# Attention stage of a hybrid decoder layer on eight cores: the dilation groups in reverse order, the value blocks spread to the end, the normalisation by token blocks

## The chip, the cores and the metric

One Trainium2 chip; the same program runs on 8 cores, each on its own 2048 of the 16384 tokens, with the 2048 tokens ahead of them as a halo. No data passes between the cores. The time is the device time of the slowest core in microseconds. Engines: PE is TensorE (PEld its weight loads), DVE is VectorE, ACT is ScalarE, POOL is GpSimd, SP is SyncE, which only starts transfers.

## The reference, cut to what matters

Three groups of four heads attend with a window of 128, 512 or 2048 positions and a dilation of 1, 4 or 16: each query sees 129 keys of its own residue stream. The three groups are merged by their softmax denominators, which is one sum of numerators over one sum of denominators.

```
ATTN_GROUPS = ((128, 1), (512, 4), (2048, 16))  # (window, dilation) per head group
...
        for gi, (window, dilation) in enumerate(ATTN_GROUPS):
            hs = slice(gi * HEADS_PER_GROUP, (gi + 1) * HEADS_PER_GROUP)
            o_g, lse_g = dilated_window_attention(q[:, :, hs], k[:, :, hs], v[:, :, hs], window, dilation)
...
        wts = jax.nn.softmax(jnp.stack(lses, axis=0), axis=0)  # (G, B, S, Hg)
        o_attn = jnp.sum(wts[..., None] * jnp.stack(outs, axis=0), axis=0)
        y_pool = multiscale_pool(u, w_pool_mix[l], pool_scale[l])
        merged = gate_a * (o_attn @ w_proj_attn[l]) + gate_p * (y_pool @ w_proj_pool[l])
        x = x + rms_norm(merged @ w_out[l], g_post_mix[l])
```

A SwiGLU feed-forward layer follows.

## The kernel before, in words

The program is written out by hand: `pe.op`, `act.op`, `dve.op` and `pool.op` put an instruction at the end of their engine's own list, each engine runs its list in that order, and `waits=` makes an instruction wait for events of others. So an instruction that waits holds up all that stands behind it on its engine.

The stages of a core, in order: load and normalise x (`own_tick`), transpose it to `hT`; keys and queries with rotary embedding (`rope_unit`: eight matmuls at L438, a copy on ACT, a rotation matmul at L482, two products on DVE at L485 and L487, a sum on POOL at L498 into `qT` or `kT`, laid out by residue stream, so that POOL reads its inputs with a step of 4 or 16 elements for the dilated groups); the attention stage; the gated merge (L925 to L947); the output projection with its norm (L988); the feed-forward layer (L1144 to L1176).

The attention stage is the loop over `u`. A **unit** is a group `g`, a part `s_`, a half and a head pair `pr`; there are 48, 16 for each group. Step `u` of the loop puts out:

- `att_scores(u)`: 8 score matmuls into one of two bank pairs (L770), the exponential on ACT into a tile `PT` (L774, 128x1024), the mask product on DVE (L779).
- some **value blocks** (`v_own`: 8 matmuls at L518 in one of two banks, an eviction on ACT at L522), taken from `v_list` in the order of the groups.
- parts of the pooling branch: window sums and means of channel half 0 on DVE (`c0_steps`), window sums of half 1 on POOL in two runs of four instructions (`h10[0]`, `h11[0]`), their means on DVE (`h10[1]`, `h11[1]`, L709), and `pool_mix`, one matmul (L731) and one ACT instruction (L733).
- `att_apply(u - 2)`: 12 matmuls (L792, L797) into one of two banks; the first group is then copied into `acc` by ACT (L812), the others are added to `acc` by DVE (L815). The next use of that bank waits for this.

`acc` holds numerator and denominator in token order, so the dilated groups write it with a step of 4 or 16 floats. `att_norm` turns one pair's denominators of 512 tokens into reciprocals by a logarithm and an exponential on ACT (L830, L831) and multiplies (L832) into `oT2`, which the merge reads. The buffer `PT2` and `acc` lie where rope's tables, its temporaries and its weights were; therefore ACT and DVE wait ahead of the stage for all of PE's, DVE's and POOL's rope work.

## Time and profile before

| | |
|---|---|
| median of 3 runs | 1025.14 us (1024.16 to 1026.15) |
| the profiled execution, its own time | 1024.68 us |
| its span, on core 2, the slowest | 1023.1 us (the other cores from 1013.3) |
| PE busy | 930.6 us, 91% of the span |
| DVE, ACT, POOL busy | 39%, 33%, 33% |
| chain that ended last | PE 80%; DVE 5%; DMA 4%; issue 4%; POOL 3%; ACT 3% |
| attention stage on core 2 | from the first value matmul at 222.07 us to the first merge matmul at 336.22 us |

The span runs from the first to the last instruction of the slowest core; the device time is 1.6 us longer. PE is busy for nearly all of the second half; the stages in which it isn't are the first 110 us and the attention stage. "PEclk" is the clock granted to TensorE as a share of the full one (2.4 GHz; the lower level is 1.2 GHz).

### The profile page before, as it was taken

Reading aid. Unit: us, or ns where it says so; the run is one execution under the profiler, and the core shown is the slowest. Engines: PE = TensorE matmul, PEld = TensorE weight load, DVE = VectorE, ACT = ScalarE, POOL = GpSimd, SP = SyncE. Lnnn points to the kernel's source line nnn. Section 1 sums busy time; section 2 is a strip of 40 time slices with the busy share of each in tenths; the row PEclk is TensorE's granted clock in tenths of the full one; section 3 lists DMA queues with packets and bytes.
Section 4 is the critical chain, followed back from the end, with each engine's and each line's share of the span. In section 5 each row is a group of like instructions: output and inputs, shape, how many; then the busy total and the mean of one; then the engine's idle time right before and its main releaser. Section 6 shows DMA issues by size and latency. Waiting matters only on the chain.

```text
span 1023.1 us, 15111 instructions; the slowest of 8 cores (1013.3 to 1023.1 us)
## 1 busy us (share of the span) xinstructions
PE 930.6 (91%) x5448; PEld 468.4 (46%) x5532; DVE 402.5 (39%) x554; ACT 342.2 (33%) x588; POOL 334.7 (33%) x324
## 2 busy tenths in 40 slices
PE   1569999999897999999898999999999999999993
PEld 0337554447674444444444444444444444444441
DVE  2465786548978433333576212121112112121111
ACT  3426663339777422223664111111101111111100
POOL 2462787663402343333456111111333000000331
PEclk9769999999998999999999999999999999999997
DMA  8879310000022171212977766762334544530322
GB/s 233 243 173 239 80 63 21 1 1 2 4 41 43 43 124 21 42 21 42 304 240 194 118 108 117 122 108 49 124 105 139 86 71 74 83 62 1 124 104 81
DMA packets 32586, 98.50 MB, mean 96 GB/s; under 512 B 4224, under 2 KB 4224, under 8 KB 32512
## 3 DMA queue, kind: packets, MB, share of 16 engines
q0 software_dynamic: 15296, 41.92, 24.8%
q1 hardware_dynamic: 17072, 55.58, 16.3%
q8 instruction: 45, 0.74, 0.3%
q14 instruction: 29, 0.24, 0.1%
q10 hardware_dynamic: 144, 0.03, 0.0%
HBM read 122.64 MB, written 16.78 MB: 136 GB/s over the span
## 4 chain that ended last, share of the span: by engine, by line
PE 80%; DVE 5%; DMA 4%; issue 4%; POOL 3%; ACT 3%; SPq 0%; DVEq 0%; ACTq 0%; POOLq 0%
PE ps L1176 14%; PE ps L1147 14%; PE ps L1144 14%; PE ps L438 12%; PE ps L925 6%; PE ps L928 5%; PE ps L518 5%; DMA xst<-xh 2%; PE ps L988 2%; PE ps L420 2%; PE ps L935 1%; PE ps L932 1%; PE ps L482 1%; DMA xin<-xo 1%; DVE tb L996 1%
## 5 line engine op out<-in xcount | busy, mean ns | idle before, releaser
L1144 PE MATMUL ps<-hT,wgu 128*128 128x512 bf16 x658 | 157.5, 379 | 1.5 <-DMA wgu<-wgu 0.7
L1147 PE MATMUL ps<-hT,wgu 128*128 128x512 bf16 x659 | 157.6, 379 | 0.7
L1176 PE MATMUL ps<-wdn,ffT 128*128 128x512 bf16 x690 | 151.5, 379 | 2.6 <-DVE ffT L1159 1.9
L1159 DVE TENSOR_TENSOR ffT<-ps,sa 128x512 bf16<-128x512 f32 x88 | 60.8, 691 | 226.2 <-PE ps L1147 226.2
L1158 ACT ACTIVATE sa<-ps 128x512 f32<-128x512 f32 x88 | 52.5, 597 | 247.3 <-PE ps L1144 247.3
L1176 PEld LDWEIGHTS ps<-wdn,ffT 128*128 128x128 bf16 x704 | 68.8, 98 | 85.4 <-issue 2.8
L1144 PEld LDWEIGHTS ps<-hT,wgu 128*128 128x128 bf16 x672 | 65.6, 98 | 79.8 <-issue 1.2
L1147 PEld LDWEIGHTS ps<-hT,wgu 128*128 128x128 bf16 x672 | 65.8, 98 | 79.3
L74 POOL DMA_DIRECT2D wgu<-wgu x42 | 22.5, 537 | 231.9 <-PE ps L1147 228.3
L1001 POOL TENSOR_TENSOR x1b<-tb,xin 128x1024 f32<-128x1024 f32 x31 | 72.8, 2348 | 58.3 <-DVE tb L996 29.9
L438 PE MATMUL ps<-hT,wqk 128*128 128x512 bf16 x374 | 89.4, 379 | 2.0 <-DVE uh L631 1.4
L498 POOL TENSOR_TENSOR kT<-t,t2b 128x512 bf16<-128x512 f32 (+1 forms) x36 | 65.4, 1826 | 47.3 <-DVE t2b L487 43.6
L359 ACT ACTIVATE junk<-ps 128x1024 bf16<-128x1024 f32 x31 | 31.7, 1022 | 142.4 <-PE ps L1176 132.4
L996 DVE SCALAR_TENSOR_TENSOR tb<-ps,rsA,gfin 128x1024 f32<-128x1024 f32 x15 | 19.3, 1284 | 131.2 <-POOL rsA L343 131.2
L947 POOL TENSOR_TENSOR mT<-m,m 128x512 bf16<-128x512 f32 x32 | 40.5, 1266 | 86.9 <-DVE m L942 86.9
L508 ACT ACTIVATE qb<-ps 128x512 bf16<-128x512 f32 (+1 forms) x60 | 35.0, 584 | 89.8 <-PE ps L438 88.2
L925 PE MATMUL ps<-hT,wgs 128*128 128x512 bf16 x249 | 60.5, 386 | 0.5 <-issue 0.2
L928 PE MATMUL ps<-hT,wgs 128*128 128x512 bf16 x250 | 60.4, 380 | 0.3
L420 PE MATMUL ps<-ident,xsb 128*128 128x128 bf16 x256 | 23.8, 249 | 40.2 <-ACT xsb L407 22.4
L941 DVE TENSOR_TENSOR m<-ps,sga 128x512 f32<-128x512 f32 x32 | 22.1, 692 | 93.6 <-PE ps L932 88.0
L438 PEld LDWEIGHTS ps<-hT,wqk 128*128 128x128 bf16 x384 | 37.1, 98 | 44.0 <-issue 1.3
L988 PE MATMUL ps<-wout,mT 128*128 128x512 bf16 x249 | 56.7, 379 | 0.4
(120 smaller groups left out, 1195.8 us busy)
## 6 DMA issues: line engine op xcount, KB each, us to landing
wgu<-wgu POOLq DMA_DIRECT2D x42, 512.0 KB, 5.1
xst<-xh SPq DMA_DIRECT2D x16, 512.0 KB, 18.0
xin<-xo SPq DMA_DIRECT2D x16, 512.0 KB, 5.4
x1s<-x1b SPq DMA_DIRECT2D x16, 512.0 KB, 3.9
xin<-x1s SPq DMA_DIRECT2D x16, 512.0 KB, 4.1
out<-x1b SPq DMA_DIRECT2D x15, 512.0 KB, 2.9
...
```

Of the source, the lines that this page charges most:

```text
L438: ev = pe.op(lambda e, k=k: e.matmul(ps[:, bank, 0:n], lhsT=wfn(k), rhs=rhsfn(k), start=(k == 0), stop=(k == 7)), signal=(k == 7))
L498: ev_o = pool.op(lambda e: e.tensor_tensor(out=dst, in0=i0, in1=i1, op=ALU.add), waits=[ev_t1, ev_t2])
L518: ev = pe.op(lambda e, k=k: e.matmul(ps[:, bank, 0:256], lhsT=tok_ap_fn(k), rhs=wv_tile[:, g, k, :], start=(k == 0), stop=(k == 7)), signa ...
L925: e1 = pe.op(lambda e, k=k, wb=wb, b1=b1, tok=tok: e.matmul(ps[:, b1, :], lhsT=wgs[wb][:, 0, k, :], rhs=hT[:, k, tok], start=(k == 0), sto ...
L928: e2 = pe.op(lambda e, k=k, wb=wb, b2=b2, tok=tok: e.matmul(ps[:, b2, :], lhsT=wgs[wb][:, 1, k, :], rhs=hT[:, k, tok], start=(k == 0), sto ...
L988: ev = pe.op(lambda e, k=k, hf=hf, pr_=pr_: e.matmul(ps[:, pr_[0] + hf, :], lhsT=mT[:, k, i * 128:(i + 1) * 128], rhs=wout[:, k, hf * 512: ...
L1001: ev_o = pool.op(lambda e: e.tensor_tensor(out=outbuf[:, :], in0=tb[b][:, :], in1=xres[:, :], op=ALU.add), waits=[ev_t, ev_xres, out_free])
L1144: e1 = pe.op(lambda e, k=k, wbuf=wbuf, ba=ba, tok=tok: e.matmul(ps[:, ba, :], lhsT=wbuf[:, 0, k, :], rhs=hT[:, k, tok], start=(k == 0), st ...
L1147: e2 = pe.op(lambda e, k=k, wbuf=wbuf, bb=bb, tok=tok: e.matmul(ps[:, bb, :], lhsT=wbuf[:, 1, k, :], rhs=hT[:, k, tok], start=(k == 0), st ...
L1158: es = act.op(lambda e, ub=ub, ba=ba: e.activation(out=sa[ub][:, :], in_=ps[:, ba, :], func=AF.Silu), waits=[e1, sa_free[ub]])
L1159: ef = dve.op(lambda e, ub=ub, bb=bb, j=j, b=b: e.tensor_tensor(out=ffT[:, j, b * 512:(b + 1) * 512], in0=ps[:, bb, :], in1=sa[ub][:, :], ...
L1176: ev = pe.op(lambda e, j=j, h2=h2, pr_=pr_, il=il: e.matmul(ps[:, pr_[0] + h2, :], lhsT=ffT[:, j, il * 128:(il + 1) * 128], rhs=wdn[:, j, ...
```

## The change

The groups come in the order 2, 1, 0 (dilation 16, 4, 1), all by part, half and pair (before, group 2 came last, first all of pair 0 and then all of pair 1). With it `v_list`, the slots of the value weights, the places of the value blocks, and the order of the last four by three rope units are turned round. One value block is put out in each step up to `u` = 44 (before, six in five steps up to 36). ACT waits for the end of rope ahead of step 2 and DVE in step 1, not ahead of the stage. The pooling branch's steps lie one to three steps later, and `pool_mix` of half 1 three steps behind its means. The first group's copy by ACT is now that of dilation 16, with a step of 16 floats, and the last group's DVE additions are contiguous. `att_norm` becomes `norm_inv` and `norm_mul` of both pairs and 512 tokens: a token block is complete after four units of group 0, so three of the four are put out in steps 38 to 48, all multiplications on DVE.

```diff
-        order = (6, 10, 7, 11, 8, 9, 0, 4, 1, 5, 2, 3) if b < 3 else (6, 0, 7, 1, 10, 8, 11, 9, 4, 5, 2, 3)
+        order = (6, 10, 7, 11, 8, 9, 0, 4, 1, 5, 2, 3) if b < 3 else (10, 4, 11, 5, 8, 2, 9, 3, 6, 0, 7, 1)
...
-    act.wait(ev_qk, dve.last(), pool.last())
-    dve.wait(ev_qk, pool.last())
+    ev_rope = [ev_qk, dve.last(), pool.last()]
...
-        if g == 0:
+        if g == 2:
             ev2 = act.op(lambda e: e.activation(out=dst, in_=src, func=AF.Copy), waits=[ev])
             acc0[0] = ev2
         else:
             ev2 = dve.op(lambda e: e.tensor_tensor(out=dst, in0=src, in1=dst, op=ALU.add), waits=[ev, acc0[0]])
-            acc_ev[pr] = ev2
+            if g == 0 and half:
+                acc_ev[(pr, s_)] = ev2
...
-    units = [(g, s_, half, pr) for g in range(2) for s_ in range(4) for half in range(2) for pr in range(2)]
-    units += [(2, s_, half, pr) for pr in range(2) for s_ in range(4) for half in range(2)]
+    units = [(g, s_, half, pr) for g in (2, 1, 0) for s_ in range(4) for half in range(2) for pr in range(2)]
...
-    def att_norm(pr, b, eng):
+    norm_ev = {}
+
+    def norm_inv(b):
         tok = slice(b * 512, (b + 1) * 512)
...
+        ev_ln = act.op(lambda e: e.activation(out=acc[:, 1, :, tok], in_=acc[:, 1, :, tok], func=AF.Ln), waits=[acc_ev[(0, b)], acc_ev[(1, b)]])
+        norm_ev[b] = act.op(lambda e: e.activation(out=acc[:, 1, :, tok], in_=acc[:, 1, :, tok], func=AF.Exp, scale=-1.0), waits=[ev_ln])
+
+    def norm_mul(b):
+        tok = slice(b * 512, (b + 1) * 512)
+        ev_oT[b] = dve.op(lambda e: e.tensor_tensor(out=oT2[:, :, tok], in0=acc[:, 0, :, tok], in1=acc[:, 1, :, tok], op=ALU.mult),
+                          waits=[norm_ev[b], acc_ev[(0, b)], acc_ev[(1, b)], ev_q2])
...
     for u in range(-1, len(units) + 2):
+        if u == 2:
+            act.wait(*ev_rope)
         if 0 <= u < len(units):
             att_scores(u)
...
-        while nv < min(len(v_list), 6 * (u + 4) // 5):
+        while nv < min(len(v_list), u + 4):
             v_own(*v_list[nv])
             nv += 1
-        if 0 <= u < 8:
-            c0_steps[u]()
-            if u == 7:
+        if 1 <= u < 9:
+            dve.wait(*ev_rope)
+            c0_steps[u - 1]()
+            if u == 8:
                 ev_z0.append(dve.last())
                 for f in h10[0]:
                     f()
-        if 9 <= u < 13:
-            pool_mix(0, u - 9)
-        if u in (13, 14):
-            h10[1][u - 13]()
-            if u == 14:
+        if 12 <= u < 16:
+            pool_mix(0, u - 12)
+        if u in (14, 15):
+            h10[1][u - 14]()
+            if u == 15:
                 for f in h11[0]:
                     f()
-        if u in (20, 21):
-            h11[1][u - 20]()
-        if 22 <= u < 26:
-            pool_mix(1, u - 22)
+        if u in (21, 22):
+            h11[1][u - 21]()
+        if 25 <= u < 29:
+            pool_mix(1, u - 25)
...
-        if u >= 41 and u % 2 == 1 and u < 48:
-            att_norm(0, (u - 41) // 2, pool)
-    for b in range(4):
-        att_norm(1, b, dve if b % 2 == 0 else pool)
+        if u >= 38 and u % 4 == 2 and u < 50:
+            norm_inv((u - 38) // 4)
+        if u >= 40 and u % 4 == 0:
+            norm_mul((u - 40) // 4)
+    norm_inv(3)
+    norm_mul(3)
```

ACT's list at the start of the attention stage, before: the eviction of the first value block carries the wait for the other engines' rope work (`vA` is a value block, `PT` an exponential's output, the names in brackets the engines waited for).

```order
L649 ACTIVATE X_52_94<-ps 128x512 [waits p_tensor]
L522 ACTIVATE vA_17_59<-ps 128x256 [waits p_tensor,p_vector,p_gpsimd]
L522 ACTIVATE vA_17_59<-ps 128x256 [waits p_tensor] x2
L774 ACTIVATE PT_59_101<-ps 128x1024 [waits p_tensor]
L522 ACTIVATE vA_17_59<-ps 128x256 [waits p_tensor]
L774 ACTIVATE PT_60_102<-ps 128x1024 [waits p_tensor]
```

The same place after the change.

```order
L649 ACTIVATE X_52_94<-ps 128x512 [waits p_tensor]
L522 ACTIVATE vA_17_59<-ps 128x256 [waits p_tensor] x3
L773 ACTIVATE PT_59_101<-ps 128x1024 [waits p_tensor]
L522 ACTIVATE vA_17_59<-ps 128x256 [waits p_tensor]
L773 ACTIVATE PT_60_102<-ps 128x1024 [waits p_tensor]
L522 ACTIVATE vA_17_59<-ps 128x256 [waits p_tensor]
L773 ACTIVATE PT_61_103<-ps 128x1024 [waits p_vector,p_gpsimd,p_tensor]
```

The wait has moved behind five value evictions and two exponentials.

ACT's list in the last group, before: the last value block, then exponentials with the first two normalisations (L830, L831) between them.

```order
L522 ACTIVATE vA_18_60<-ps 128x256 x2
L774 ACTIVATE PT_60_102<-ps 128x1024
L774 ACTIVATE PT_62_104<-ps 128x1024
L774 ACTIVATE PT_59_101<-ps 128x1024
L774 ACTIVATE PT_60_102<-ps 128x1024
L774 ACTIVATE PT_62_104<-ps 128x1024
L830 ACTIVATE acc_100<-acc_100 128x512
L831 ACTIVATE acc_100<-acc_100 128x512
L774 ACTIVATE PT_59_101<-ps 128x1024
L774 ACTIVATE PT_60_102<-ps 128x1024
```

The same engine after the change, around the second token block's normalisation (now L831 and L832).

```order
L773 ACTIVATE PT_59_101<-ps 128x1024
L522 ACTIVATE vA_18_60<-ps 128x256
L831 ACTIVATE acc_100<-acc_100 128x2x512
L832 ACTIVATE acc_100<-acc_100 128x2x512
L773 ACTIVATE PT_60_102<-ps 128x1024
L522 ACTIVATE vA_18_60<-ps 128x256
L773 ACTIVATE PT_62_104<-ps 128x1024
L522 ACTIVATE vA_18_60<-ps 128x256
```

The normalisations are half as many and twice as large, and value evictions stand between the exponentials nearly to the end.

PE's list in the last group, before: scores (L770) and two kinds of apply matmuls, no value blocks.

```order
L770 MATMUL ps<-qT_58,kT_15_57 128x128 x8
L792 MATMUL ps<-PT_60_102,vA_19_61 64x128 x2
L792 MATMUL ps<-PT_60_102,vA_18_60 64x128 x2
L797 MATMUL ps<-PT_60_102,onesb_52 64x256 x4
L770 MATMUL ps<-qT_58,kT_15_57 128x128 x8
```

The same engine after the change, in the last group.

```order
L769 MATMUL ps<-qT_58,kT_13_55 128x128 x8
L518 MATMUL ps<-wvr_63,hT_54 128x256 x8
L791 MATMUL ps<-PT_62_104,vA_18_60 64x128 x8
L796 MATMUL ps<-PT_62_104,onesb_52 64x256 x4
L769 MATMUL ps<-qT_58,kT_13_55 128x128 x8
```

Eight value matmuls stand in each step there, up to step 44.

## Rows read from the trace of the kernel before

**Rows 1.** Stretches of the attention stage: engines' busy time, PEclk, DMA share, GB/s.

```profile
222.07:336.22 114.15, 98.14 (x1349) 70.94 (x1353) 90.91 (x101) 83.55 (x130) 29.59 (x18) 0.93 0.11 20
...
222.07:246.01 23.94, 21.80 (x269) 15.26 (x268) 15.84 (x21) 18.24 (x31) 3.37 (x2) 0.93 0.01 2
269.69:288.70 19.01, 15.39 (x180) 10.81 (x182) 15.84 (x17) 10.91 (x17) 3.75 (x3) 0.82 0.31 57
312.43:336.22 23.79, 14.16 (x246) 9.02 (x246) 20.18 (x25) 15.40 (x19) 6.43 (x6) 0.86 0.25 45
336.22:345.00 8.78, 8.78 (x33) 3.66 (x33) 3.25 (x5) 7.38 (x12) 2.54 (x2) 0.81 0.05 11
```

**Rows 2.** Waits in all, 222 to 345 us: total us, times, longest.

```profile
PE ps L792 <- DVE acc L815: 7.4, 9, 1.7
PE ps L792 <- DVE zT L709: 3.2, 1, 3.2
PE ps L518 <- ACT vA L522: 2.1, 1, 2.1
PE ps L770 <- ACT PT L774: 2.0, 1, 2.0
```

**Rows 3.** PE's instructions in order of time: start, duration, what.

```profile
237.65 0.40 PE L770 MATMUL ps<-qT,kT 64*128 64x128 bf16 x8
...
239.52 0.40 PE L770 MATMUL ps<-qT,kT 64*128 64x128 bf16 x8
...
242.27 0.40 PE L770 MATMUL ps<-qT,kT 64*128 64x128 bf16 x8
...
291.49 0.40 PE L770 MATMUL ps<-qT,kT 64*128 64x128 bf16 x8
...
293.41 0.40 PE L770 MATMUL ps<-qT,kT 64*128 64x128 bf16 x8
...
317.93 0.40 PE L770 MATMUL ps<-qT,kT 64*128 64x128 bf16 x8
...
319.47 0.40 PE L770 MATMUL ps<-qT,kT 64*128 64x128 bf16 x8
```

**Rows 4.** ACT's instructions in a step of the first group with a mix.

```profile
254.16 1.02 ACT L774 ACTIVATE PT<-ps 128x1024 bf16<-128x1024 f32 x1
255.06 0.40 ACT L522 ACTIVATE vA<-ps 128x256 bf16<-128x256 f32 x1
255.33 0.71 ACT L733 ACTIVATE zT<-ps,cpk 128x512 bf16<-128x512 f32 x1
255.90 0.63 ACT L812 ACTIVATE acc<-ps 128x512 f32<-128x512 f32 x1
256.37 1.06 ACT L774 ACTIVATE PT<-ps 128x1024 bf16<-128x1024 f32 x1
```

**Rows 5.** POOL's window sums of half 1, second run, its last two.

```profile
267.42 2.17 POOL L701 TENSOR_TENSOR Y<-Z 128x1033 f32<-128x1033 f32 x1
269.74 2.62 POOL L704 TENSOR_TENSOR Z<-Y 64x1025 f32<-64x1025 f32 x1
```

**Rows 6.** DVE in the same stretch.

```profile
265.81 4.33 DVE L779 TENSOR_TENSOR PT<-PT,masks 128x1024 bf16<-128x1024 bf16 x2 [0.30 <-ACT PT L774]
...
271.07 1.84 DVE L779 TENSOR_TENSOR PT<-PT,masks 128x1024 bf16<-128x1024 bf16 x1
```

**Rows 7.** Groups by line and shape, 222 to 345 us: count, busy, mean ns, idle before.

```profile
L815 DVE TENSOR_TENSOR acc<-ps,acc 128x512 f32<-128x512 f32 x32 | 34.6, 1086 | 3.4 <-PE ps L797 3.2
...
L693 DVE TENSOR_TENSOR Y<-X 128x1039 f32<-128x1039 f32 x2 | 2.5, 1234 | 0.0
...
L941 DVE TENSOR_TENSOR m<-ps,sga 128x512 f32<-128x512 f32 x1 | 0.7, 691 | 2.2 <-ACT sga L939 2.2
...
L498 POOL TENSOR_TENSOR qT<-t,t2b 128x512 bf16<-128x512 f32 x2 | 4.2, 2128 | 0.0
```

**Rows 8.** ACT at the first normalisation.

```profile
321.97 0.63 ACT L830 ACTIVATE acc<-acc 128x512 f32<-128x512 f32 x1 [2.51 <-DVE acc L815]
```

More of the change, by code:

```diff
@@ L517, in v_block @@
         for k in range(8):
-            ev = pe.op(lambda e, k=k: e.matmul(ps[:, bank, 0:256], lhsT=tok_ap_fn(k), rhs=wv_tile[:, g, k, :], start=(k == 0), stop=(k == 7)),
+            ev = pe.op(lambda e, k=k: e.matmul(ps[:, bank, 0:256], lhsT=tok_ap_fn(k), rhs=wv_tile[:, 2 - g, k, :], start=(k == 0), stop=(k == 7)),
                        signal=(k == 7))
@@ L530, in blk_idx @@
         if g == 0:
-            return 48 if m == 0 else m - 1
+            return 48 if m == 0 else 31 + m
         if g == 1:
             return 49 + s_ if m == 0 else 16 + 4 * s_ + (m - 1)
-        return 53 + s_ if m == 0 else 32 + s_
+        return 53 + s_ if m == 0 else s_
     def k_halo(tab, g, e0, n, t0=0):
@@ L826, in build_program @@
     ev_oT = {}
[L828 removed]
+    norm_ev = {}
+    def norm_inv(b):
         tok = slice(b * 512, (b + 1) * 512)
[L830 to L836 removed]
+        ev_ln = act.op(lambda e: e.activation(out=acc[:, 1, :, tok], in_=acc[:, 1, :, tok], func=AF.Ln), waits=[acc_ev[(0, b)], acc_ev[(1, b)]])
[4 more added lines that the diff above has]
+                          waits=[norm_ev[b], acc_ev[(0, b)], acc_ev[(1, b)], ev_q2])
+    wpa = P.sb("wpa", [128, 2, D], BF16, R_V)
+    wpp = P.sb("wpp", [128, 2, D], BF16, R_V + 4 * KB)
     wgs = [P.sb("wgs%d" % i, [128, 2, 8, 128], BF16, R_ST + 8 * KB + i * 4 * KB) for i in range(2)]
@@ L843, in build_program @@
     c0_steps = h00[0] + h00[1] + h01[0] + h01[1]
-    v_list = [(0, 0, 1 + n) for n in range(16)] + [(1, n // 4, 1 + n % 4) for n in range(16)] + [(2, n, 1) for n in range(16)]
+    v_list = [(2, n, 1) for n in range(16)] + [(1, n // 4, 1 + n % 4) for n in range(16)] + [(0, 0, 1 + n) for n in range(16)]
     nv = 0
@@ L874, in build_program @@
             att_apply(napp)
+            if napp == 15:
+                ev_g2 = pe.last()
             napp += 1
-        if u == 37:
-            assert nv == len(v_list)
-            ev_v = pe.last()
+        if u == 29:
             wg_ev = [pool.dma(wgs[i][:, :, :, :], wg_d[i], d_wg[i], waits=[ev_wz[1]]) for i in range(2)]
-            pool.dma(wpa[:, :, :], wpa_d[:, :, :], d_wm2, waits=[ev_v])
+            pool.dma(wpa[:, :, :], wpa_d[:, :, :], d_wm2, waits=[ev_g2])
             ev_wp = pool.dma(wpp[:, :, :], wpp_d[:, :, :], d_wm2)
-        if u >= 41 and u % 2 == 1 and u < 48:
-            att_norm(0, (u - 41) // 2, pool)
-    for b in range(4):
-        att_norm(1, b, dve if b % 2 == 0 else pool)
+        if u >= 38 and u % 4 == 2 and u < 50:
[4 more added lines that the diff above has]
+    norm_mul(3)
+    assert nv == len(v_list) and len(ev_oT) == 4
     tap("hT", hT[:, :, :])
@@ L929, in build_program @@
                            signal=(k == 7))
+            pe.wait(ev_oT[b])
             for p_ in range(2):
-                pe.wait(ev_oT[(p_, b)])
                 e3 = pe.op(lambda e, p_=p_, c=c, b3=b3, tok=tok: e.matmul(ps[:, b3, :], lhsT=wpa[:, p_, c * 128:(c + 1) * 128], rhs=oT2[:, p_, tok],
```

13 lines of the change are left out of this document (3 added, 10 removed).

## The prediction

> **What bounds the kernel now.** I read the page first: PE is busy 91% of the span and carries 80% of the chain that ended last, so only stages in which it waits can give time back; the change touches one of them, the attention stage. So the stage's table by stretches comes next. From the first value matmul to the merge it takes 114.15 us, with PE busy 98.14 and a granted clock of 0.93 [rows 1]. What would it take if PE never waited and never lost its clock? PE's order of time gives it. A step with one value block takes 239.52 - 237.65 = 1.87 us (1.92 later on, 293.41 - 291.49, when the block comes from hT columns 16 apart); a step with two takes 242.27 - 239.52 = 2.75 us [rows 3]. So a block is 0.88 and a bare step 0.99 us. 48 of both are 89.8; the eight mixes at 0.21 each (an estimate: 512 columns where a block has 8 x 256) and the dearer strided blocks bring it to 92. The stage loses 22 us, and the table says where:
>
> - 222.07 to 246.01: the third value block waits 2.1 us for ACT's evictions [rows 2], which stand behind rope's last POOL sum in ACT's list. Behind that wait the granted clock of the stretch is 0.93 [rows 1], which is 1.7 us. Together 3.8.
> - 269.69 to 288.70, steps 20 to 25: 19.01 us with PE busy 15.39 at a clock of 0.82. Six steps, one of them with two blocks, and four mixes are 6 x 1.89 + 0.88 + 0.84 = 13.1; lost 5.9. In it the mix waits 3.2 us for a mean on DVE [rows 2].
> - 312.43 to 336.22, steps 37 to 47, which have no value blocks: 23.79 us. PE's work is 11 x 0.99 and two more applies (estimated at 0.57 each, a little over half of a bare step), 12.0; lost 11.8. A step takes 319.47 - 317.93 = 1.54 us [rows 3], which is DVE's mask and addition; most of the 7.4 us of waits for the addition lie here, and the first normalisation holds ACT 2.51 us until DVE has added [rows 2, 8], behind which PE waits 2.0 us for an exponential. The clock is 0.86.
>
> 3.8 + 5.9 + 11.8 = 21.5; the stretch left out, 246.01 to 269.69, has the small rest.
>
> **The change part by part.**
>
> *Start.* Nothing that ACT does before step 2 waits for rope now, and rope's last POOL sums are the contiguous ones, so POOL ends no later. The 2.1 us go, and with them the fall of the clock, 1.7. The exponential's table load stays and holds the third scores by some 0.3. **-3.5.** From both sides: nothing of the clock comes back (-2.1), or all (-3.8).
>
> *Values to the end.* The 48 blocks cost the same. But eight steps that took 1.54 us without a block now have one behind which DVE's work disappears: DVE's mask is 0.69 and its contiguous addition of group 0 is like that of L941, 691 ns, not 1086 [rows 7]; 1.4 us against 1.87. ACT in such a step has 0.90 + 0.27 (starts in rows 4). The normalisations add 2 x 1.05 us on ACT every fourth step (128x512 takes 0.63 [rows 8], 128x1024 I take like the exponential's 1.02 [rows 4]). Steps 38 and 42 leave ACT 0.6 to 0.7 us free each, and the scores have two bank pairs: the delayed exponential ends about 2.9 us after its scores began and is needed two steps, 3.7 us, after; no wait on PE. They wait for an addition issued one step earlier, long done by the time ACT reaches them, which is what the 2.51 us of [rows 8] was about. The multiplication costs DVE 1.23 (L693 is as large and as contiguous [rows 7]) every fourth step, hidden as well. What remains is the tail without blocks, steps 45 to 47: `norm_inv(2)` stands ahead of the last exponential, counted from scores(45): scores(46) at +1.0, its exponential done at +2.4 (0.5 for the scores, 0.9), logarithm and inverse at +4.8 with their gaps, exponential 47 at +5.8, its mask at +6.5, addition 45, which is behind it in DVE's list, at +7.2, the last apply and with it the merge's start at +8.1. PE's work there is 3 x 0.99 + 2 x 0.57 = 4.1; lost 4.0 instead of 11.8. **-7.8.** Bounds: nothing lost (-11.8); or every one of the three normalisations costs PE what the first did before, 2.0 us and the clock, -3.
>
> *Pooling branch.* POOL's two runs still lie between steps 9 and 13 and between 16 and 21. While one runs, DVE's mask product ends 0.55 us after the POOL instruction ends: POOL's L704 ends at 272.36 and the mask that started at 271.07 at 272.91; two masks take 4.33 [rows 5, 6]. So DVE gives one mask for each POOL instruction (2.2 to 2.6 us) where PE wants one in 1.9. In group 2 DVE has slack for that. In the second run three additions of 1.1 us [rows 7] and then two means, about as long as L693's 1.23, meet it. Following DVE's list from step 16: additions 16 to 21 end 8.5, 10.8, 13.5, 16.5, 19.6 and 21.3 us after step 16's scores; the applies that reuse their banks want them at 8.9, 10.8, 12.7, 15.4, 18.4, and 21.7. PE loses 0.8 + 1.1 + 1.2 = 3.1. The mix no longer waits for the means (two steps of room). 3.1 instead of 5.9: **-2.8.** Bounds: no loss (-5.9); the same loss, with the clock falling (0).
>
> *ACT's copy with a step of 16 floats.* No row shows ACT writing with a step. A step's ACT work is now 0.90 + 0.27 + 0.47 (starts in rows 4), 1.65 to 1.8, and 2.2 with a mix, against PE's 1.92 and 2.13: it is nearly the bound. DVE's strided addition costs 0.39 more than the contiguous one for a read and a write [rows 7]; the copy has only the write. I take half, 0.2: the plain steps still fit, four mixes lose 0.2 each. **+0.7.** Bounds: 0 and the full 0.4, below.
>
> The Trainium skill (SBUF — State Buffer, Door 1) says that consecutive accesses of compute engines are at full speed only within a 16-byte line and that each crossing costs. It speaks against this edit, since every element lies in another line. That DVE's additions are dearer with a step agrees; that a write alone is, no run here shows. By the rule the copy would cost the full extra.
>
> *The rest.* The transfers of the merge's weights start in step 29, not 37, so no later ahead of the merge than before. The merge starts at a clock of 0.81 over its first 8.78 us [rows 1], 1.7 us lost, behind gaps of about 1 us; the tail leaves one gap of 2.5 us: I leave this as it is (0; bounds -1.7 and +1). **0.**
>
> Sum: -3.5 - 7.8 - 2.8 + 0.7 = -13.4. The profiled execution took 1024.68, so 1011.3; the median is 0.5 above it; I say **1011.5**. The other cores run the same lists and wait for no other core, so the slowest gains as much.
>
> **The rivals.**
>
> *A. The strided copy binds group 2.* For it: DVE's 0.39. A step of ACT is then 2.1 and with a mix 2.6 us against 1.92 and 2.13: 12 x 0.2 + 4 x 0.45 = 4 instead of 0.7 + 0.3. 1014.5.
>
> *B. The clock falls in the middle.* The gaps of 0.8 to 1.2 us in steps 22 to 24 come behind each other; behind the one of 3.2 the stretch had 0.82 for 19 us, 3.4 us [rows 1, 2]; I take 2.5. Against it: steps of 1.54 us with 0.99 of work, a gap of 0.55 in each [rows 3]. 1014.
>
> *C. Everything hides.* Full clock at the merge, and half of the DVE loss: 1008.
>
> *D. The other side: the copy is as slow as POOL is with a step.* POOL's strided sum takes 2128 ns [rows 7]. A step of ACT would be 0.90 + 0.27 + 2.13 = 3.3, with a mix 3.9: 12 x 1.4 + 4 x 1.75 = 24 us, 1034. It decides from 1.5 us for a copy, where ACT's excess equals the 14 us gained. Against it: ACT's instructions go by their elements alone (0.63 for 512, 1.02 for 1024 [rows 4, 8]), in PSUM or out of it.
>
> *E. The spreading doesn't do what it says:* the normalisations still block exponentials: three times 2 us and some clock, 1018.
>
> **How the numbers follow.** Main case 0.58 (1008.5 to 1013.5), A 0.17, B 0.08, C 0.07, E 0.05, D 0.03, something unseen that eats the gain 0.02. 1007 to 1017 leaves out D, E and part of C: about 0.15. A measurement of this kernel tells 0.2% from nothing, about 2 us; below 1023 lie all cases but D and the unseen: faster 0.94, same 0.02, slower 0.04; since lists followed miss things, I give 0.91, 0.04, 0.05.
>
> **What would show it.** Right: the first scores about 2.7 us after the first value matmul, and no wait of PE on ACT's evictions; steps of 1.9 us at full clock throughout group 0; waits on DVE's additions only around the end of POOL's second run, some 3 us; the merge 101 us after the first value matmul; L811 at 0.6 to 0.8 us. Wrong: L811 at 1.0 or more with PE waiting for exponentials in group 2; a clock under 0.95 between steps 20 and 30; gaps at steps 40 and 44; a merge that starts earlier but runs longer.

## The result and the profile after the change

The changed kernel takes 1016.7 us as the median of four executions, 0.992 of the kernel before (95% interval 0.990 to 0.994), which ran at 1024.9 us beside it. That is 8.2 us faster and 5.2 us above the forecast; the range given, 1007 to 1017, holds it by 0.3 us. One of the four (1181.4 us) met a slower state of the chip, which executions of any kernel here can meet; the other three took 1016.0 to 1017.0 with a median of 1016.4, and the medians below leave such executions out. The profiled execution took 1016.38 us, with core 0 the slowest.

The page, its first line, PE's row, and the granted clock in 40 slices:

```profile
span 1014.8 us, 15184 instructions; the slowest of 8 cores (1008.9 to 1014.8 us)
...
PE 934.0 (92%) x5532; PEld 466.2 (46%) x5532; DVE 395.0 (39%) x556; ACT 344.0 (34%) x580; POOL 327.2 (32%) x318
...
PEclk9879999999997999999999999999999999999997
```

The stage by stretches, from the first value matmul to the merge and its first 8.75 us (columns as in [rows 1]):

```profile
217.50:323.85 106.35, 94.67 (x1354) 67.93 (x1352) 83.32 (x103) 87.91 (x128) 22.63 (x14) 0.97 0.13 22
217.50:242.45 24.95, 24.70 (x339) 19.30 (x337) 17.84 (x24) 23.41 (x36) 3.41 (x3) 1.00 0.01 1
242.45:253.74 11.29, 8.72 (x118) 6.00 (x117) 8.82 (x7) 11.29 (x18) 7.66 (x4) 1.00 0.01 1
253.74:274.91 21.17, 17.39 (x256) 12.67 (x254) 17.96 (x22) 15.45 (x24) 10.68 (x7) 1.00 0.01 2
274.91:313.31 38.40, 38.40 (x566) 26.57 (x565) 30.27 (x41) 31.48 (x46) 0.89 (x2) 1.00 0.35 57
313.31:323.85 10.54, 5.46 (x87) 3.39 (x85) 8.43 (x13) 6.28 (x8) 0.00 (x0) 0.74 0.01 2
323.85:332.60 8.75, 8.75 (x32) 3.50 (x31) 3.69 (x5) 4.74 (x6) 0.86 (x1) 0.73 0.25 82
```

These borders are the scores of steps 12, 16, 25 and 45. The reader sees three different rows. At the start and from step 25 to 45 PE is busy all the time at full clock. In steps 12 to 15 it is busy 8.72 of 11.29 us and ACT for all 11.29. Behind step 45 PE is busy half the time, and the clock falls to 0.74 and stays low into the merge. The stage takes 106.35 us where [rows 1] had 114.15.

The waits that answer to [rows 2], over 215 to 332 us:

```profile
PE ps L791 <- DVE acc L814: 8.2, 9, 2.3
...
ACT acc L831 <- DVE acc L814: 5.7, 3, 3.8
...
PE ps L518 <- ACT vA L522: 2.0, 4, 0.5
...
PE ps L730 <- ACT vA L522: 1.0, 1, 1.0
```

The waits for an addition come to 8.2 us where they were 7.4, nine times in both, and the single wait of 3.2 us for a mean is gone. The 2.0 us on ACT's eviction are four waits of 0.5, in steps 13 to 16, no longer one at the start; the 1.0 us is the mix of step 12, which waits for ACT too. The last of the four:

```profile
254.62 1.04 PE L518 MATMUL ps<-wvr,hT 128*128 128x256 bf16 x8 [0.48 <-ACT vA L522]
```

**Forecast and measured by stretch** (us, core 0; the forecast as the prediction's terms give it: steps 12 to 15 are 4 x (1.92 + 0.21 + 0.2), steps 16 to 24 are 9 x 1.9 + 3.1, steps 25 to 44 are 20 x 1.87 + 4 x 0.21):

| | forecast | after |
|---|---|---|
| first value block to scores(3) | 7.4 | 7.67 |
| scores(3) to scores(12) | 17.3 | 17.28 |
| scores(12) to scores(16) | 9.3 | 11.29 |
| scores(16) to scores(25) | 20.2 | 21.17 |
| scores(25) to scores(45) | 38.2 | 38.40 |
| scores(45) to the merge | 8.1 | 10.54 |

Two stretches make 4.4 us of the miss, one between them 1.0. The merge's first step then takes 6.62 us, where it was 5.78 on core 2 before; at full clock it is 4.32.

### The profile page after: what moved, and what is told of

Same layout as the page of the kernel before. It is cut to its first block, busy times and chain, and to the rows that moved or that the text cites. A ratio compares the mean times of both kernels' runs of the same rounds, so it can differ in the third digit from the quotient of the medians.

```text
span 1014.8 us, 15184 instructions; the slowest of 8 cores (1008.9 to 1014.8 us)
## 1 busy us (share of the span) xinstructions
PE 934.0 (92%) x5532; PEld 466.2 (46%) x5532; DVE 395.0 (39%) x556; ACT 344.0 (34%) x580; POOL 327.2 (32%) x318
## 4 chain that ended last, share of the span: by engine, by line
PE 83%; DVE 4%; issue 3%; DMA 3%; ACT 3%; POOL 1%; SPq 0%; DVEq 0%; ACTq 0%; POOLq 0%
PE ps L1185 15%; PE ps L1153 14%; PE ps L1156 14%; PE ps L438 12%; PE ps L934 6%; PE ps L937 6%; PE ps L518 5%; PE ps L997 2%; PE ps L420 2%; DMA xst<-xh 1%; PE ps L944 1%; PE ps L941 1%; PE ps L791 1%; PE ps L769 1%; DMA xin<-xo 1%
## 5 line engine op out<-in xcount | busy, mean ns | idle before, releaser
L934 PE MATMUL ps<-hT,wgs 128*128 128x512 bf16 x256 | 62.2, 387 | 0.0
L937 PE MATMUL ps<-hT,wgs 128*128 128x512 bf16 x256 | 61.1, 382 | 0.0
L773 ACT ACTIVATE PT<-ps 128x1024 bf16<-128x1024 f32 x48 | 54.6, 1144 | 12.2 <-PE ps L769 12.2
```

What stands on the lines that cost most here:

```text
L773: ev_e = act.op(lambda e: e.activation(out=PT[k3][:, :, :], in_=ps[:, b0:b0 + 2, :], func=AF.Exp, scale=0.125), waits=[ev, pt_free[k3]])
L934: e1 = pe.op(lambda e, k=k, wb=wb, b1=b1, tok=tok: e.matmul(ps[:, b1, :], lhsT=wgs[wb][:, 0, k, :], rhs=hT[:, k, tok], start=(k == 0), sto ...
L937: e2 = pe.op(lambda e, k=k, wb=wb, b2=b2, tok=tok: e.matmul(ps[:, b2, :], lhsT=wgs[wb][:, 1, k, :], rhs=hT[:, k, tok], start=(k == 0), sto ...
```

## The experiments

The first value matmul comes at 213 to 223 us depending on the core and the execution, and what follows the merge's start varies by 2 to 6 us between the cores; the stage itself is alike on the cores within 0.1 to 0.5 us in most kernels after the change. So two lengths of the trace stand beside the times: the stage, and the stretch from the first value matmul to the fourth merge step, which also holds what the stage hands on. Both are medians of the 8 cores.

| kernel | median us | of the before beside it, interval | stage | to 4th merge step |
|---|---|---|---|---|
| before | 1024.9 | | 113.1 | 128.4 |
| after | 1016.4 | 0.992, 0.990 to 0.994 | 106.4 | 121.6 |
| e_contig | 1015.4 | 0.990, 0.987 to 0.993 | 105.4 | 119.8 |
| e_start | 1019.9 | 0.994, 0.992 to 0.997 | 109.4 | 124.1 |
| e_startw | 1019.9 | 0.994, 0.992 to 0.996 | 107.9 | 122.3 |
| e_nopool2 | 1013.8 | 0.989, 0.986 to 0.991 | 104.0 | 118.6 |
| e_tail | 1014.1 | 0.989, 0.987 to 0.992 | 102.6 | 115.9 |
| e_mixlate | 1019.4 | 0.995, 0.993 to 0.997 | 106.2 | 121.5 |
| e_norev | 1020.0 | 0.995, 0.993 to 0.997 | 103.0 | 122.0 |
| e_vfast | 1024.0 | 0.998, 0.996 to 0.999 | 110.0 | 124.8 |
| e_step4 | 1018.3 (one run) | | 108.0 | 122.1 |
| e_step2 | 1015.5 (one run) | | 105.4 | 119.4 |
| e_best2 | 1010.6 | 0.986, 0.984 to 0.988 | 101.6 | 114.6 |
| e_best3 | 1013.4 | 0.989, 0.987 to 0.991 | 103.7 | 116.6 |

**e_contig: the copy written contiguously.** Numerators and denominators of group 2 don't land in token order, so the output is not the layer's.

```diff
-            src = ps[:, bank, :].rearrange("p (n r a) -> p n r a", n=2, r=2)
...
-            dst = acc[:, :, pr, :].rearrange("p n (a r) -> p n r a", r=16)[:, :, r0:r0 + 2, :]
+            dst = acc[:, :, pr, r0 * 128:(r0 + 2) * 128]
```

> The changed kernel, but the copy of the first group (dilation 16) writes 256 consecutive floats of acc, not every 16th: it leaves out that these sums stand in token order, so its output is not the layer's. Theory 1, the step of the copy costs ACT 0.35 us each and binds group 2: the copy's start to the next start is 0.47 to 0.50 us and not 0.83, steps 12 to 16 take 8.8 us and not 11.3, step 16 0.2 to 0.5 less, nothing else moves, and the time is 2.5 to 3.5 us below the changed kernel's 1016.7. Rival, POOL's first run of window sums (it lies over the same steps) holds DVE's masks and PE: steps 12 to 16 stay at 11 us and the time within 0.7 us of the changed kernel's.

ACT's order of time in the changed kernel:

```profile
239.71 0.64 ACT L522 ACTIVATE vA<-ps 128x256 bf16<-128x256 f32 x1
239.96 1.36 ACT L811 ACTIVATE acc<-ps 128x512 f32<-128x512 f32 x1
240.78 1.39 ACT L773 ACTIVATE PT<-ps 128x1024 bf16<-128x1024 f32 x1
...
246.63 1.46 ACT L811 ACTIVATE acc<-ps 128x512 f32<-128x512 f32 x1
247.49 1.45 ACT L773 ACTIVATE PT<-ps 128x1024 bf16<-128x1024 f32 x1
```

and in e_contig:

```profile
241.10 0.60 ACT L810 ACTIVATE acc<-ps 128x512 f32<-128x512 f32 x1
241.60 1.02 ACT L773 ACTIVATE PT<-ps 128x1024 bf16<-128x1024 f32 x1
```

From start to next start the stepped copy holds ACT for 0.82 to 0.86 us, the contiguous one for 0.47 to 0.50. Steps 12 to 15 fall from 11.29 to 9.37 us, so ACT's copy was their bound. But steps 16 to 24 grow from 21.17 to 22.07, and the stage gains 1.0 us, not the 2.5 to 3.5 expected of the time. Nearly half of the 1.9 us is handed back: PE reaches step 16 1.9 us sooner, but POOL's second run, which waits for DVE's means of half 0, starts only 0.9 us sooner (38.6 us after the first value matmul, not 39.5), and scores(25) comes behind it.

**e_step4 and e_step2: how the price of a step depends on its size.** Here too the numbers lie in other places and the output is not the layer's. The first new line is that of e_step4, the second that of e_step2:

```diff
-            dst = acc[:, :, pr, :].rearrange("p n (a r) -> p n r a", r=16)[:, :, r0:r0 + 2, :]
...
+            dst = acc[:, :, pr, r0 // 8 * 1024 + r0 // 2 % 4:r0 // 8 * 1024 + 1024:4]
...
+            dst = acc[:, :, pr, r0 // 4 * 512 + r0 // 2 % 2:r0 // 4 * 512 + 512:2]
```

> The changed kernel with ACT's copy of group 2 written with a step of 4 floats (16 bytes) in place of 16 floats; the numbers land in the wrong places, so the output is not the layer's. With step 16 the copy occupies ACT 0.82 to 0.86 us from start to next start, contiguous 0.47 to 0.49, and steps 12 to 16 take 11.3 and 9.37 us. Theory 1 (a cost for each 16-byte line that a write enters: every element in another line with a step of 4 as of 16): 0.82 to 0.86 us, steps 12 to 16 in 11.3 us, additions after it as before. Theory 2 (the cost grows with the distance): 0.55 to 0.7 us, steps 12 to 16 in 9.4 to 10.4 us.

> The same with a step of 2 floats (8 bytes), two elements to a 16-byte line; the output again is not the layer's. Theory 1 (cost for each line entered; contiguous enters one for 4 elements, step 2 one for 2, steps 4 and 16 one for each): of the extra 0.35 us a third, 0.12, so 0.6 us from start to next start; a step of ACT with a mix is then 2.25 us and steps 12 to 16 take 9.4 to 9.7 us. Rival (any write that is not contiguous pays all): 0.82 to 0.86 us and 11.3 us.

ACT in e_step4, then in e_step2:

```profile
242.28 1.40 ACT L810 ACTIVATE acc<-ps 128x512 f32<-128x512 f32 x1
243.19 1.35 ACT L773 ACTIVATE PT<-ps 128x1024 bf16<-128x1024 f32 x1
```

```profile
242.08 0.66 ACT L810 ACTIVATE acc<-ps 128x512 f32<-128x512 f32 x1
242.62 1.01 ACT L773 ACTIVATE PT<-ps 128x1024 bf16<-128x1024 f32 x1
```

With 16 bytes between elements the copy holds ACT 0.86 to 0.91 us and steps 12 to 15 take 11.7; with 8 bytes it holds it 0.55 and they take 9.37, as contiguous. Each of the two kernels ran once. So the price doesn't grow from 16 bytes to 64, and is nearly absent at 8. The theory that the distance sets it fell, and so did the one that any step pays all. The Trainium skill (SBUF — State Buffer, Door 1) says that full speed needs at least two accesses to the same 16-byte line. The traces agree: with a step of 8 bytes two elements share a line and the copy costs 0.05 us more than contiguous, with 16 and 64 bytes none do and it costs 0.35 more. An estimate that shares the extra out by lines entered would make 8 bytes 0.6 us, a little too much.

**e_start and e_startw: the start.** e_startw puts only the wait for rope back ahead of the stage, for ACT and DVE; e_start also restores the last four by three rope units' old order.

```diff
     ev_rope = [ev_qk, dve.last(), pool.last()]
+    act.wait(*ev_rope)
+    dve.wait(*ev_rope)
...
-        if u == 2:
-            act.wait(*ev_rope)
```

> The changed kernel with the start as before: ACT and DVE wait for rope ahead of the stage, and the last four by three rope units are in the old order, the contiguous ones first. Theory, the term of the prediction: the third value block waits 2.1 us and the clock falls behind it, 3 to 4 us more from the first value matmul to the fourth scores, time 3 to 4 us above the changed kernel. Rival: the wait comes back but nothing of the clock is lost on the way, 2.1 us.

> The changed kernel with only the waits for rope put back ahead of the stage; the rope units stay in the new order. POOL's last rope sum ends 2.4 us after the first value matmul there, not 3.4. Theory: the third value block waits 1.0 us, the clock does not fall, 1.0 to 1.3 us more in all; so the order of the rope units, not the place of the wait alone, gives more than half of the term. Rival: the place of the wait is all of it, 3 to 4 us more.

ACT's first value eviction in e_start, then in e_startw:

```profile
217.46 0.66 ACT L522 ACTIVATE vA<-ps 128x256 bf16<-128x256 f32 x2 [2.95 <-POOL qT L498]
```

```profile
219.35 0.66 ACT L522 ACTIVATE vA<-ps 128x256 bf16<-128x256 f32 x2 [1.88 <-POOL qT L498]
```

The stretch to scores(3) is 7.67 us in the changed kernel, 9.00 in e_startw and 10.0 (cores 4 to 7) or 11.2 (cores 0 to 3) in e_start. The wait costs 1.3 us behind the contiguous rope sums and 2.4 or 3.5 behind the stepped ones. The two figures differ by the clock: the third value block waits 2.22 us on core 0 and 2.19 on core 4, but the granted clock of the stretch is 0.85 on cores 0 to 3 and 1.00 on cores 4 to 7. In e_startw it is 1.00 on all. Once the wait is moved, the order no longer matters: e_norev below, with the old order, has 7.62, in group 0 with its blocks of 0.88 us.

**e_nopool2: without POOL's second run.** Its four window sums are left out, and with them the means' wait for their last, so the means of its second token half come from the sums of the first, and the output is not the layer's.

```diff
-            if u == 15:
-                for f in h11[0]:
-                    f()
```

> The changed kernel without POOL's second run of four window sums; it leaves that part of the pooling branch out (the means take what stands in the buffers). Theory, DVE's masks wait for the end of POOL's instructions: steps 16 to 25 take 18 to 18.8 us and not 21.2 (only the two means of 1.27 us are left over what DVE has free), masks in steps 18 to 20 take 0.7 us, the time is 2.3 to 3.2 us lower. Rival, DVE is simply full there with masks, additions and means: steps 16 to 25 stay above 20.5 us and the time within 0.8 us of the changed kernel.

Steps 16 to 24 fall from 21.15 to 18.77 us, the rest of the stage stays. What costs the 2.4 us is seen in the changed kernel at POOL's last sum and the mask that meets it:

```profile
264.21 2.62 POOL L703 TENSOR_TENSOR Z<-Y 64x1025 f32<-64x1025 f32 x1
```

```profile
265.54 1.85 DVE L778 TENSOR_TENSOR PT<-PT,masks 128x1024 bf16<-128x1024 bf16 x1
```

The mask's work is 0.69 us; it ends at 267.39, 0.56 behind the end of POOL's instruction, as in [rows 5, 6].

**e_mixlate: the mixes of half 0 in steps 29 to 32, not 12 to 15.**

```diff
-        if 12 <= u < 16:
-            pool_mix(0, u - 12)
+        if 29 <= u < 33:
+            pool_mix(0, u - 29)
```

> The changed kernel with the four mixes of channel half 0 in steps 29 to 32, not 12 to 15. Theory 1, ACT is the bound of these steps (0.95 + 0.26 + 0.57 + 0.83 = 2.6 us against PE's 2.13): steps 12 to 16 take 8.1 to 8.4 us and not 11.3, the four later steps 0.2 us more each, time 2.0 to 2.8 us lower. Rival, POOL's first run and the masks bind: no gain there, time within 0.7 us.

Steps 12 to 15 take 9.37 us, steps 16 to 24 22.08, steps 25 to 36 24.25 instead of 23.39: the stage gains 0.2 us, nothing, where a time 2.0 to 2.8 us lower was expected. Without mixes PE's own pace would be 4 x 1.92 = 7.7, so something else binds at 9.37. PE's waits there:

```profile
246.26 0.41 PE L791 MATMUL ps<-PT,vA 128*64 128x128 bf16 x8 [0.36 <-DVE PT L778]
...
248.58 0.41 PE L791 MATMUL ps<-PT,vA 128*64 128x128 bf16 x8 [0.36 <-DVE PT L778]
...
251.36 0.41 PE L791 MATMUL ps<-PT,vA 128*64 128x128 bf16 x8 [0.82 <-DVE PT L778]
```

PE waits for masks, and one mask comes for each sum of POOL's first run. The sums take 2.36, 2.18, 2.18 and 2.63 us and start 2.50, 2.32 and 2.32 us apart; PE's steps 12 to 15 take 1.97, 2.32, 2.32 and 2.77. So beneath ACT's bound lies the first run's, 1.7 us over PE's pace without mixes and 0.85 over it with them. No run leaves the first run out; that it is this bound is read from these times and waits.

**e_tail: the normalisation of block 2 behind the last exponential,** the multiplications 1 to 3 at the end. Nothing is left out.

```diff
-        if u >= 38 and u % 4 == 2 and u < 50:
-            norm_inv((u - 38) // 4)
-        if u >= 40 and u % 4 == 0:
-            norm_mul((u - 40) // 4)
+        if u in (38, 42):
+            norm_inv((u - 38) // 4)
+        if u == 40:
+            norm_mul(0)
+    norm_mul(1)
+    norm_inv(2)
     norm_inv(3)
+    norm_mul(2)
     norm_mul(3)
```

> The changed kernel with the third token block's logarithm and inverse behind the last exponential on ACT, and the multiplications of blocks 1 to 3 behind the last addition on DVE. Theory, the tail of 10.5 us from scores(45) to the merge is made by what stands ahead of the last exponential (two instructions of 1.05 us, which themselves wait for additions behind a multiplication of 1.2 us): the tail takes 6 to 7 us, the merge's first step at the full clock or nearly, time 3.5 to 5.5 us lower. Rival 1, DVE's mask and addition bind the tail anyway: under 1.5 us lower. Rival 2, the later sigmoids of the merge (behind three normalisations, 6.4 us and a table load) hold up its third step and give it back.

The changed kernel's tail, PE, then ACT, then DVE:

```profile
313.31 0.40 PE L769 MATMUL ps<-qT,kT 64*128 64x128 bf16 x8
314.71 0.41 PE L791 MATMUL ps<-PT,vA 128*64 128x128 bf16 x8 [1.00 <-DVE acc L814]
...
315.28 0.40 PE L769 MATMUL ps<-qT,kT 64*128 64x128 bf16 x8
...
318.24 0.64 PE L791 MATMUL ps<-PT,vA 128*64 128x128 bf16 x8 [1.37 <-DVE acc L814]
...
322.85 0.64 PE L791 MATMUL ps<-PT,vA 128*64 128x128 bf16 x8 [2.34 <-DVE acc L814]
...
323.85 3.59 PE L934 MATMUL ps<-hT,wgs 128*128 128x512 bf16 x8
```

```profile
310.05 1.06 ACT L831 ACTIVATE acc<-acc 128x1024 f32<-128x1024 f32 x1 [0.54 <-DVE acc L814]
...
312.16 1.00 ACT L773 ACTIVATE PT<-ps 128x1024 bf16<-128x1024 f32 x1
...
318.19 1.06 ACT L831 ACTIVATE acc<-acc 128x1024 f32<-128x1024 f32 x1 [1.39 <-DVE acc L814]
...
320.30 1.00 ACT L773 ACTIVATE PT<-ps 128x1024 bf16<-128x1024 f32 x1
```

```profile
313.27 0.69 DVE L778 TENSOR_TENSOR PT<-PT,masks 128x1024 bf16<-128x1024 bf16 x1 [2.11 <-ACT PT L773]
313.88 0.68 DVE L814 TENSOR_TENSOR acc<-ps,acc 128x512 f32<-128x512 f32 x1
...
315.68 1.21 DVE L836 TENSOR_TENSOR oT<-acc 128x1024 bf16<-128x1024 f32 x1
...
321.41 0.69 DVE L778 TENSOR_TENSOR PT<-PT,masks 128x1024 bf16<-128x1024 bf16 x1 [2.11 <-ACT PT L773]
322.02 1.28 DVE L814 TENSOR_TENSOR acc<-ps,acc 128x512 f32<-128x512 f32 x2
```

Read it backwards. The merge waits for the last apply, that for an addition behind the last mask (321.41), that for the last exponential (320.30), that for the logarithm and inverse ahead of it in ACT's list (318.19), and the logarithm 1.39 us for an addition that stands behind the multiplication of block 1 on DVE (315.68). Ahead of it stands a first wait, 1.00 us at 314.71. It has another source: the exponential at 312.16 stands behind block 1's normalisation on ACT (310.05, its logarithm 0.54 us late for an addition itself), its mask on DVE waits for it until 313.27, and the addition that PE wants stands behind that mask (313.88).

In e_tail the chain is gone, and the first wait is not; the same place on PE:

```profile
313.84 0.41 PE L791 MATMUL ps<-PT,vA 128*64 128x128 bf16 x8 [1.00 <-DVE acc L814]
...
318.67 0.41 PE L791 MATMUL ps<-PT,vA 128*64 128x128 bf16 x8 [0.57 <-DVE acc L814]
...
319.24 1.90 PE L937 MATMUL ps<-hT,wgs 128*128 128x512 bf16 x8
```

From scores(45) to the merge 6.79 us, not 10.54, and the first merge step takes 4.33 at full clock. On cores 4 to 7 the third merge step then takes 4.7 to 5.2, the sigmoids being late behind two more normalisations. To the fourth merge step 5.7 us are gained; the medians differ by 2.3. The edit moves block 2's two ACT instructions and the multiplications together, so it doesn't share the 3.75 us of the tail out between them.

**e_norev: the old order of the groups** 0, 1, 2, and of rope with it, the pairs side by side, the value blocks still one in each step, the waits still moved, all four normalisations at the end, since in this order no token block is complete sooner.

```diff
-    units = [(g, s_, half, pr) for g in (2, 1, 0) for s_ in range(4) for half in range(2) for pr in range(2)]
+    units = [(g, s_, half, pr) for g in (0, 1, 2) for s_ in range(4) for half in range(2) for pr in range(2)]
...
-        if g == 2:
+        if g == 0:
             ev2 = act.op(lambda e: e.activation(out=dst, in_=src, func=AF.Copy), waits=[ev])
```

> The changed kernel with the groups in the old order (dilation 1, 4, 16, both pairs side by side), with all else kept: one value block in each step, the later wait for rope, the later pooling steps; all four token blocks are normalised behind the last unit, since none is complete before. It computes the whole layer. Theory, what gained time is the spreading of the value blocks, not the reversal: no step ahead of 45 is bound by ACT or a stepped copy (3 us less), the tail without normalisations is 5 to 6 us and not 10.5 (5 less), and the merge gives back 2 to 4 us, since its first projection waits for the first block (3.5 us behind the last addition) and its sigmoids for 8.4 us of normalisation; time 3 to 6 us below the changed kernel. Rival, the reversal is needed: the stepped additions (1.05 against 0.69 us) bind the last group or the merge stalls for more than 8 us, time at or above the changed kernel's.

The stage is 3.3 us shorter than the changed kernel's (steps 12 to 15 in 9.74, the tail in 7.1 to 8.0), but to the fourth merge step it is 122.0 against 121.6, and the time is 3.6 us above the changed kernel's, not 3 to 6 below. The merge pays. ACT, then PE:

```profile
327.32 1.06 ACT L831 ACTIVATE acc<-acc 128x1024 f32<-128x1024 f32 x1
328.40 1.28 ACT L944 ACT_TABLE_LOAD   x1
```

```profile
331.89 1.89 PE L930 MATMUL ps<-hT,wgs 128*128 128x512 bf16 x8 [2.28 <-DVE m L947]
```

Four normalisations hold ACT until 328.38, the sigmoids come behind them, and the merge's banks come free 2.28 us late.

**e_vfast: six value blocks in five steps again,** in the new order.

```diff
-        while nv < min(len(v_list), u + 4):
+        while nv < min(len(v_list), 6 * (u + 4) // 5):
```

> The changed kernel with six value blocks in five steps as before, so that none is left from step 37 on. Theory, the term of the prediction: steps 37 to 44 take 1.3 to 1.5 us of DVE and ACT work against 0.99 of PE work and two normalisations now block them, 4 to 6 us are lost there, and ACT-bound group 2 gives 1 us back; time 3 to 5 us above the changed kernel. Rival, the contiguous additions of group 0 alone (0.68 us) already took away what bound the last group: under 1.5 us above.

Against the changed kernel the stretches change by +1.3, +1.7, -1.3, 0.0, +2.5 and -0.6 us up to scores(45), and the tail not at all: 3.6 us longer, and the time 7.6 us above the changed kernel's where 3 to 5 were expected. Of the eight blocks of steps 37 to 44 three now fall ahead of step 12 and three in steps 25 to 36, at about 0.9 us each. Two fall in steps 16 to 24, where PE waits anyway, and cost nothing; steps 12 to 15 have as many as before and get 1.3 us cheaper. The steps that they leave get only 0.6 us cheaper together: they then take 1.80 us each without a block, waiting for additions and for exponentials behind a normalisation.

**e_best2 and e_best3: the findings put together.** Both have e_tail's tail. e_best2 puts the mixes of half 0 in steps 20 to 23, into PE's waits for DVE. e_best3 puts them in 16 to 19 and the branch's second half later.

```diff
-        if 12 <= u < 16:
-            pool_mix(0, u - 12)
+        if 20 <= u < 24:
+            pool_mix(0, u - 20)
```

```diff
-            if u == 15:
-                for f in h11[0]:
-                    f()
-        if u in (21, 22):
-            h11[1][u - 21]()
-        if 25 <= u < 29:
-            pool_mix(1, u - 25)
+        if u == 30:
+            for f in h11[0]:
+                f()
+        if u in (36, 37):
+            h11[1][u - 36]()
+        if u in (39, 40, 41, 43):
+            pool_mix(1, min(u, 42) - 39)
```

> The changed kernel with the normalisation of block 2 behind the last exponential, the multiplications 1 to 3 at the end, and the four mixes of half 0 in steps 20 to 23 in place of 12 to 15. The tail as in the run with the tail alone: 6.8 us from scores(45) to the merge and a first merge step of 4.33. The mixes: steps 12 to 16 in 9.37 us (11.3), steps 16 to 25 in 22.1 (the same as with the mixes in group 1, if their 0.84 us of PE lies in PE's waits for DVE) or 22.9 (if not), steps 25 to 37 in 23.4. Theory: stage 102.6 - 1.9 + 0.9 = 101.6, about 1013. Rival, the stretch 16 to 25 is set by PE and not by DVE's lag: 102.4, no gain over the tail alone.

> The changed kernel with the same tail, the mixes of half 0 in steps 16 to 19, and the second run of POOL's window sums at step 30 (means in 36 and 37, mixes in 39 to 41 and 43, the merge's weights requested in step 38): there DVE's additions are contiguous, 0.69 us in place of 1.1. Theory (POOL's run costs where DVE has no slack: a step of DVE is 1.8 of 1.92 us in group 1 and 1.4 of 1.87 in group 0): steps 12 to 16 in 9.4, 16 to 25 in 18.9 (as without the run, 18.77, plus little for the mixes), 25 to 37 and 37 to 45 together 38.4 plus about 1; stage 102.6 - 1.9 - 2.2 + 1 = 99.5, time about 1011. Rival (the run costs the same 2.4 us wherever it lies, since DVE gives one mask for each POOL instruction): 100.9 to 102, time 1012.5 to 1013.5; and the later weights may hold the merge.

e_best2 does what was expected: 9.37, 22.08, 23.39 and 6.79 us, the stage 101.6, the time 1010.6, 15 us under the kernel before beside it (1025.6) and 5.8 under the changed one. Its stage on core 3, the clock in the third column from the end:

```profile
215.90:317.50 101.60, 93.37 (x1353) 67.32 (x1351) 84.37 (x101) 88.14 (x128) 22.62 (x14) 1.00 0.15 23
```

e_best3 misses, and its expectation rested on a mistake of mine. POOL, DVE, ACT and PE there:

```profile
255.67 2.36 POOL L692 TENSOR_TENSOR Y<-X 128x1039 f32<-128x1039 f32 x1 [5.53 <-DVE zT L712]
```

```profile
296.89 1.28 DVE L708 SCALAR_TENSOR_TENSOR zT<-Z,cpk,X 64x1024 bf16<-64x1024 f32 x1
```

```profile
298.99 1.06 ACT L831 ACTIVATE acc<-acc 128x1024 f32<-128x1024 f32 x1 [1.24 <-DVE acc L814]
```

```profile
302.53 1.03 PE L518 MATMUL ps<-wvr,hT 128*128 128x256 bf16 x8 [2.27 <-ACT vA L522]
```

POOL starts its second run at 255.67, as early as ever: nothing in its own list holds it but the means of half 0, so the step in which it is written down doesn't matter. Only the means on DVE moved. Steps 16 to 24 fall to 20.1 us for that (22.08 in e_best2, with mixes in either). In group 0 the means put DVE behind, the first logarithm waits 1.24 us for an addition, value evictions and exponentials stand behind it on ACT, and PE waits 2.27 us; with the clock's fall behind it on five of the cores (0.92 on core 0, 1.00 on core 2), steps 37 to 44 take 20.7 us there and 19.1 on the others, in place of 15.0.

## Why the prediction was right, and where its sizes were off

**How near.** The time came out in the range with 0.3 us to spare and the gain at 8.2 of the 13.4 us forecast. The mechanisms named were mostly the true ones, but two terms were mis-sized in the same direction, the tail and the stepped copy, and a third by less, the pooling branch. Of the signs, the first scores at 2.7, full clock in the middle and steps of 1.9 in group 0 came. The merge 101 us after the first value matmul did not (106.35). Two signs of being wrong came: L811 was recorded at 1.34 us with PE waiting for ACT in group 2, if for evictions and hardly for exponentials, and the merge started earlier but ran longer.

**Start, -3.5.** Right. The first scores come 2.72 us after the first value matmul, forecast 2.7, and the stretch to scores(3) takes 7.67 us against a forecast of 7.4. Putting back wait and rope order costs 2.4 us on four cores and 3.5 on the other four (e_start), so the full term needs the clock's fall and only the 2.1 us of the wait is sure. The rope order, which the prediction took for no term, matters only to a wait that is no longer there.

**Values to the end, -7.8.** The mechanism was right: with a block in each step group 0 runs at 1.88 us for a step and full clock, 38.40 us with PE busy 38.40, and taking the blocks forward again costs 3.6 us (e_vfast). The step that failed is the tail, "the merge's start at +8.1": it came at +10.54. I followed ACT's list and held the awaited additions for "long done". They were late for two reasons. Counted from scores(45), scores(46) started at +1.97, not +1.0, behind a wait of 1.00 us for an addition. That is block 1's normalisation on ACT: the exponential behind it ended 3.6 us after its scores and not 2.9, and the addition stands behind that exponential's mask in DVE's list. I had checked only that the exponential itself was in time; e_tail, which has the multiplication of block 1 at the end, has the same wait and scores(46) at +1.96. Then the logarithm started at +4.9 after 1.39 us more of waiting, and here the multiplication of 1.21 us does stand ahead of the awaited addition on DVE. The rest of the chain ran with the lengths foretold. e_tail takes block 2's normalisation and the multiplication out of it and the tail is 6.79. By the stretches the term came to -5.3: from scores(37) to the merge it was 23.79 us with no value block and is 25.55 with eight of 0.88, so 18.5 without them, where -7.8 would have given 16.0.

**The merge, 0.** The first merge step is 6.62 us, 0.8 above core 2's of before, inside the bound of +1 (all cores: 5.9 to 6.7, before 5.3 to 6.7). That this comes of the tail's gaps is shown by e_tail: 4.33.

**Stepped copy, +0.7.** Mis-sized by the choice of "half, 0.2". It is 0.35 us, the full extra, with 0.05 more for each exponential behind it (0.95 us from start to next start, 0.90 in e_contig), and rival A's mechanism is the true one. ACT's step was 2.04 us in the plain steps against PE's 1.92. That didn't show there, since exponentials may lag by two steps, so steps 3 to 11 kept 1.92; it fell due in steps 12 to 15, where ACT's step is 2.6: they take 11.29 us, 2.0 above the forecast, and step 16 another 0.5 (its value block waits 0.48 us for ACT). Cost against the contiguous copy: 1.9 us in place, 1.0 net (e_contig). So rival A priced it too high, at 3.3 us over the main case, and that its 1014.5 lies nearer to the time than 1011.5 is in part luck.

**Pooling branch, -2.8.** Steps 16 to 24 lose 4.1 us instead of 3.1. Of that 0.5 is ACT's, in step 16; steps 20 to 24 lose 3.6, with PE waiting 3.3 us for additions around the end of POOL's second run, as foretold. Without the second run steps 16 to 24 lose 1.7 (18.77 against 17.1), ACT's 0.5 in it. The wrong sentence is "In group 2 DVE has slack for that". DVE had, but the sequence didn't: one mask for each POOL instruction is a pace of 2.32 us for PE, and steps 12 to 15 went below 9.37 in no kernel with the branch's new steps (e_contig, e_step2, e_mixlate, e_best2 all end there, by different edits). In the changed kernel this costs nothing yet, since ACT's bound of 11.29 lies above it.

**Why single repairs bring little.** Steps 12 to 24 have three bounds on top of each other: ACT, POOL's first run, then DVE with POOL's second run. A gain at the first arrives at the last as a longer wait: 1.9 us became 1.0 in e_contig and 0.2 in e_mixlate, which also moved 0.84 us of PE work into steps with no gap. e_best2 moved the same work into gaps and kept the 1.0.

**What each part is worth,** by the length to the fourth merge step: moved waits and rope order 2.5 us, spread values 3.2; the reversed order with the normalisation by blocks 0.4, which is nothing. It shortens the merge's start and lengthens the stage by the same. That is of the normalisation as placed here; with e_tail's placement the reversed order is 6.1 us ahead of e_norev, whose own normalisation nobody tried to place better. The three parts are 6.1 of the 6.8 us; the pooling branch's later steps were put back in no run, and what they gave stays open.

**What stays open.** The medians don't follow the lengths in each kernel. The four that ran on one chip (e_tail, e_mixlate, e_norev, e_vfast) are all 3 to 4 us dearer against the changed kernel than their lengths to the fourth merge step say; the others, on another chip, are dearer too, by 0.4 to 1.4 us, but for e_startw (2.8) and e_best3 (2.0). The kernel before took 1024.9 us beside the changed one, 1025.9 beside the four, and 1024.9 and 1025.6 beside the others, which is up to 1.0 us of it. In the profiled executions the median core of the four spends 673.5 to 675.0 us behind that step (the others 672.4 to 674.4) against 672.6 in the changed kernel, which is another part. Of the 8.2 us between before and after 6.8 lie in that length, and the other 1.4 are as open. No run separates chip, order of execution and the stages behind. What is said above of the parts goes by the lengths.
